# A chunked RWKV-7 scan: the state kept as 128x64 without its zero blocks, with the products on it made per head

## What is computed

```python
    def step(S, inp):
        r_t, k_t, v_t, kk_t, a_t, w_t = inp
        sa = jnp.einsum('bhij,bhj->bhi', S, kk_t)
        S = (S * w_t[:, :, None, :] - sa[..., None] * (kk_t * a_t)[:, :, None, :]
             + v_t[..., None] * k_t[:, :, None, :])
        return S, jnp.einsum('bhij,bhj->bhi', S, r_t)
```

## Time and profile before

| | |
|---|---|
| median of 3 runs | 2623.42 us (2622.43 to 2625.33) |
| profiled execution | 2622.69 us |
| its span | 2620.5 us |
| mean granted TensorE clock | 0.946 |
| TensorE busy | 2308.7 us (88%) |
| VectorE busy | 1187.0 us (45%) |
| ScalarE busy | 790.7 us (30%) |
| GpSimd busy | 441.7 us (17%) |

### The profile page before, as it was taken

The page is one execution under the profiler, slowest core; times in us unless marked ns, Lnnn a source line. Parts: engine busy times, 40 slices in busy tenths (PEclk is TensorE's granted clock), DMA queues, the critical chain, the costliest instruction groups (busy, mean ns, idle before and its releaser), DMA issues. The chain is left out here.

```text
span 2620.5 us, 51046 instructions
## 1 busy us (share of the span) xinstructions
PE 2308.7 (88%) x21174; PEld 2102.2 (80%) x21174; DVE 1187.0 (45%) x2330; ACT 790.7 (30%) x1494; POOL 441.7 (17%) x239
## 2 busy tenths in 40 slices
PE   5999999999999999999999789999246637999996
PEld 4998989898988888899999777888223327999996
DVE  4244545444454545348898144444223425443223
ACT  4343333333332332122222344544111113232111
POOL 0000000000000000001100499999200000000000
PEclk8999999999999999999999899999668877999998
DMA  3321222222221212268775513221575632342232
GB/s 116 98 83 60 83 64 75 64 79 60 80 79 60 80 62 85 75 198 287 226 254 186 153 57 93 69 85 44 164 236 170 189 115 103 124 146 106 102 101 93
DMA packets 124556, 301.65 MB, mean 115 GB/s; under 512 B 24218, under 2 KB 37156, under 8 KB 118596
## 3 DMA queue, kind: packets, MB, share of 16 engines
q1 hardware_dynamic: 97972, 242.44, 29.1%
q0 software_dynamic: 7696, 32.78, 3.6%
q10 hardware_dynamic: 18688, 23.59, 2.8%
HBM read 261.55 MB, written 45.54 MB: 117 GB/s over the span
## 5 line engine op out<-in xcount | busy, mean ns | idle before, releaser
L177 PE MATMUL acc<-xh,w_hi 128*128 128x272 f32 x3008 | 670.5, 304 | 24.0 <-DVE xl L433 12.0
L177 PE MATMUL acc<-xh,w_lo 128*128 128x272 f32 x3008 | 624.8, 289 | 0.0
L177 PE MATMUL acc<-xl,w_hi 128*128 128x272 f32 x3008 | 623.8, 289 | 0.0
L177 PEld LDWEIGHTS acc<-xh,w_hi 128*128 128x128 f32 x3008 | 472.1, 190 | 76.0 <-issue 45.4
L177 PEld LDWEIGHTS acc<-xl,w_hi 128*128 128x128 f32 x3008 | 475.7, 190 | 0.0
L177 PEld LDWEIGHTS acc<-xh,w_lo 128*128 128x128 f32 x3008 | 473.4, 190 | 0.0
L160 DVE TENSOR_TENSOR w_lo<-w_raw,w_hi 128x1024 fp32r<-128x1024 f32 x166 | 203.2, 1224 | 412.6 <-ACT w_hi L152 411.5
L152 ACT ACTIVATE w_hi<-w_raw 128x1024 fp32r<-128x1024 f32 x188 | 198.5, 1056 | 301.1 <-PE acc L177 245.7
L1171 DVE SCALAR_TENSOR_TENSOR b_C<-b_rows,b_pos_s,b_C 128x512 f32<-128x512 f32 x240 | 162.4, 743 | 0.0
L893 PE MATMUL rbank<-m 64*64 64x64 f32 x3840 | 130.9, 220 | 1.1 <-DVE m L584 1.1
L893 PEld LDWEIGHTS rbank<-m 64*64 64x64 f32 x3840 | 118.8, 135 | 15.2 <-issue 3.8
(11 more groups left out here) (386 smaller groups left out, 3350.6 us busy)
## 6 DMA issues: line engine op xcount, KB each, us to landing
w_raw<-in_w_all SPq DMA_DIRECT2D x188, 512.0 KB, 3.6
b_rows<-in_cmp_rows SPq DMA_DIRECT2D x128, 256.0 KB, 3.7
d_kv<-in_sel_kv SPq DMA_DIRECT2D x128, 256.0 KB, 2.9
m_w<-in_w_mo SPq DMA_DIRECT2D x32, 1024.0 KB, 5.7
m_gates<-tmp_uT SPq DMA_DIRECT2D x16, 544.0 KB, 3.7
out_s_win<-in_win_in POOLq DMA_DIRECT2D x8, 1016.0 KB, 5.8
tmp_uT<-ub POOLq DMA_DIRECT2D x24, 272.0 KB, 2.3
tmp_uT<-ub ACTq DMA_DIRECT2D x23, 272.0 KB, 2.6
```

The source lines that it names most:

```text
L177: ins = self.nc.tensor.matmul(acc[:, c, 0:HALF], w[:, k % KH, :], x[:, k, c * HALF:(c + 1) * HALF], start=(k == 0 and m == 0), stop=(k == ...
```

## The change

S and Sd become 128x64: head 0's state on partitions 0 to 63, head 1's on 64 to 127, in the same columns. U is made by two products of 64 rows, one per head, into two PSUM banks (0 and 1 instead of 1). The state part of O is made per head too, and each stands ahead of its head's UV part. The new S takes one VectorE instruction instead of two. The final transpose of S gives 64x128, and the stores of `p_rwkv` read it so. Banks and gaps of all other jobs stay, so the place of every background piece does.

```diff
@@ PAIR_JOBS
-    PAIR_JOBS += [(f"U{_n}", 1, 1, "dve", 2), (f"O{_n}", 3, 1, "act", 1), (f"S{_n}", 0, 1, "dve", 0)]
+    PAIR_JOBS += [(f"U{_n}", 0, 2, "dve", 2), (f"O{_n}", 3, 1, "act", 1), (f"S{_n}", 0, 1, "dve", 0)]
@@ rwkv
-        S, Sd, S_nat = sb("S", [P, P]), sb("Sd", [P, P]), sb("S_nat", [P, P])
+        S, Sd, S_nat = sb("S", [P, CH]), sb("Sd", [P, CH]), sb("S_nat", [CH, P])
@@ GpSimd
-                    pool.dma_start(A["p_rwkv"][2 * i + h], S_nat[h * HD:(h + 1) * HD, h * HD:(h + 1) * HD]).then_inc(s_sent, 16)
+                    pool.dma_start(A["p_rwkv"][2 * i + h], S_nat[:, h * HD:(h + 1) * HD]).then_inc(s_sent, 16)
@@ VectorE
-                        in0=bank[0:CH, bank_of[i, f"U{n}"], 0:P].rearrange("p (h i) -> p h i", h=2), scalar=-1.0,
+                        in0=bank[0:CH, bank_of[i, f"U{n}"]:bank_of[i, f"U{n}"] + 2, 0:CH], scalar=-1.0,
                         in1=W2[:, :, n, :], op0=ALU.mult, op1=ALU.subtract).then_inc(ev_dve, 1)
@@
-                    for h, hp in enumerate((slice(0, CH), slice(CH, P))):
-                        last = stt(out=S[hp, h * CH:(h + 1) * CH], in0=bank[hp, bank_of[i, f"S{n}"], 0:CH],
-                                   scalar=last_p[hp], in1=Sd[hp, h * CH:(h + 1) * CH], op0=ALU.mult, op1=ALU.add)
-                    last.then_inc(ev_dve, 1)
+                    stt(out=S[:, :], in0=bank[:, bank_of[i, f"S{n}"], 0:CH], scalar=last_p, in1=Sd[:, :],
+                        op0=ALU.mult, op1=ALU.add).then_inc(ev_dve, 1)
@@ ScalarE
-                out(i, "S_out", S_nat[:, :], bank[:, bank_of[i, "S_out"], 0:P])
+                out(i, "S_out", S_nat[:, :], bank[0:CH, bank_of[i, "S_out"], 0:P])
@@ TensorE
-                    done(mm(bank[0:CH, bank_of[i, f"U{n}"], 0:P], mats["W1T"][:, n, :], S[:, :], start=True, stop=True))
+                    for h, hp in enumerate(H):
+                        ins = mm(bank[0:CH, bank_of[i, f"U{n}"] + h, 0:CH], mats["W1T"][hp, n, :], S[hp, :],
+                                 start=True, stop=True)
+                    done(ins)
@@
-                    mm(bank[:, b, 0:CH], S[:, :], KR[:, n, 1, :], start=True, stop=False)
                     for h, hp in enumerate(H):
+                        mm(bank[hp, b, 0:CH], S[hp, :], KR[hp, n, 1, :], start=True, stop=False)
                         ins = mm(bank[hp, b, 0:CH], UV[:, n, h * CH:(h + 1) * CH],
                                  G[:, h, n, CH:P], start=False, stop=True)
@@
-                done(nc.tensor.transpose(bank[:, bank_of[i, "S_out"], 0:P], S[:, :], ident[:, :]))
+                done(nc.tensor.transpose(bank[0:CH, bank_of[i, "S_out"], 0:P], S[:, :], ident[:, :]))
```

## The result

| | before | changed |
|---|---|---|
| median | 2623.42 us | 2651.91 us (2648.48 to 2657.03, 5 runs) |
| profiled execution | 2622.69 us | 2654.75 us |
| span | 2620.5 us | 2652.6 us |
| mean granted TensorE clock | 0.946 | 0.944 |

The changed kernel is slower: ratio 1.0113, 95% interval 1.0099 to 1.0126 (the two medians of the table alone give 1.0109). The forecast was 2648 us, 2637 to 2660.

The account below looks back on a forecast made before the run. TensorE, busy 117.2 of 120.9 us per pair, was taken to bound the kernel. O +31.6, U -4.1 and VectorE -2.5 sum to +25.0 us, giving 2648 us, range 2637 to 2660.

Parts of the forecast that it names:

- The price of a change of tile shape: In O on TensorE: each visit to another tile shape costs 0.14 us on top of its passes.
- a case with 4 rows against 128: Sample attention's L2110 (4 rows) against L2109 (128 rows), both 64 columns: source of the 0.14 us per visit.
- The visits of 0.25 us: In O: each visit with one 64-column product takes 0.14 + 2 x 0.055 = 0.25 us.
- the +0.39: O to S in the 25 chunks where TensorE waits ahead of O: 0.39 us longer each.
- forecast 0.56: O to S in the 39 chunks without a wait ahead of O: 0.56 us longer each.
- The rival of cheap row changes: In O, changing rows alone costs nothing extra: 2621.5 us, no change; chance 0.08.
- case in between: In O, neighbouring heads overlap after all: 2632 us; lies between the forecast and the cheap-rows rival.
- The rival that the changes are dearer still: In O, each shape change costs 0.20 us with the first weights, 11.5 us more: 2660 us; chance 0.09.
- 0.50 was forecast, from five chunks: U per head saves 0.10 us in the 5 chunks a pair where the saving reaches the end.
- -0.36 a pair forecast: VectorE's single S update (-0.29 us) and smaller Sd (-0.07), on the path once a pair.
- a lower clock in the stage: A lower granted TensorE clock in the scan would make it slower than forecast; no size given.

Follow-up runs that it names:

- o_alone: Kernel before the change with only O's state part made per head (64x64), each ahead of its head's UV part: 2662.43 us, ratio 1.0156.
- states_first: Changed kernel with O's two 64x64 state products next to each other, then the two UV products: 2614.39 us, ratio 0.9972.
- split_s: Changed kernel with the state update as two VectorE instructions of 64 partitions again: 2659.26 us, ratio 1.0149.
- state_early: Changed kernel with O's two state products issued directly behind U's, in the same 64x64 tile: 2602.81 us, ratio 0.9924.
- early_gap3: Changed kernel with O's state products directly behind U's and background pieces moved to O1, O4, O5 from U2, U5, U6: 2582.71 us, ratio 0.9845.
- o_tall: Kernel before with U per head and O's state part per head over all 128 rows, zeros included: 2612.12 us, ratio 0.9963.
- gap_after: Changed kernel with one background piece per pair moved from ahead of U2 to ahead of O1: 2638.67 us, ratio 1.0052.

## Why the prediction was right

- **The price of a change of tile shape** was the step on which all rested, taken from a case with 4 rows against 128. The visits of 0.25 us came out as forecast, and o_alone gives 4.12 us a pair where 3.97 was worked out. After a wait, O to the next job took 616.06 - 614.95 = 1.11 us instead of 604.68 - 603.96 = 0.72 (the latter two starts in the kernel before): the +0.39. Without one it grew by 0.59, forecast 0.56. The rival of cheap row changes fell with it. The rule that the Trainium skill gives in "TensorEngine Tiling (Array Packing)", Tiling Modes, is that a change of tiling mode drains TensorE; this case agrees: two shape changes fewer, in states_first, gave 3.9 us a pair. The prediction's case in between, that neighbouring heads overlap after all, could not come in the order of the change; states_first shows that they do overlap once they are neighbours. The rival that the changes are dearer still (0.20 a visit) fell by the 0.25 us steps.
- **U** saved 0.54 us a pair; 0.50 was forecast, from five chunks.
- **VectorE** was mis-sized: -0.36 a pair forecast. The update in one instruction gave 0.62, by split_s, and Sd takes 0.03 less (254 ns median instead of 286; no run tries it alone). I had called the update hidden in the chunks where UV waits for w_lo, and that was wrong by 0.11 us in each of three.
- **The sum of a pair**: 4.12 - 0.54 - 0.65 = 2.93, and the changed kernel's pair measures 2.93. Forecast was 3.11 (3.97 - 0.50 - 0.36).
- **The last pair** should have been 3.2 us longer by the forecast's terms (4 x 0.56 + 4 x 0.39 - 0.6) and is 2.3 longer, from its first U to its last job. The prediction left out a fifth wait there, ahead of the final transpose of S. It was 1.3 us (first line below, the kernel before) and is 0.4 (second line, the changed kernel); in o_alone, with VectorE's work as before, it is 0.7. So TensorE's extra time was partly hidden in it, where the prediction said that none would be.

```profile
PE rbank L973 <- DVE S L605: 1.3, 1, 1.3
```

```profile
PE rbank L974 <- DVE S L604: 0.4, 1, 0.4
```

- **The clock**: the text named a lower clock in the stage as something that would make it slower than forecast, and gave it no price. It came: 3 x 1.55 = 4.7 us. With it the scan grew by 27.3 us in the profiled execution, from its first U to its last job (25.0 forecast without any low clock, 22.7 measured without it).
- **The rest**, 4.4 us behind the scan, lies in the prompt attention in this execution. What sets the clock there from run to run was not tried; the median grew by 28.5, less than this execution's 32.1.

That the forecast of 2648 lies 4 us from the median owes something to errors of opposite sign: the scan without its low clock was taken 2.3 us too dear (0.18 of it in each pair, 0.9 in the last), and the clock's 4.7 us were left out. The mechanism was right; the closeness of the number is partly luck.

## What to carry to other kernels

Smaller matmuls are not cheaper by themselves: count how often the sequence changes the array's tile shape, and read the price of one change from start to start of neighbouring rows. Put products of one shape next to each other, even if some multiply zeros. Where a wait stands in a table of gaps, try to move filler work there before cutting the work around it; here that was worth 20 us (state_early to early_gap3). state_early was itself 20 us ahead of the kernel before, of which the cheaper U and state update are about 9 and the order of the products the rest.

## What the runs showed of the hardware that was not expected

- A visit to another tile shape costs 0.14 to 0.15 us beyond its passes, whether the rows change (0.25 us from L961 to L962 for two passes that need 0.11), the columns (0.26 from L959 to L961) or both (L948, 0.15). Products of different heads in one shape overlap even across jobs (630.69 and 630.70 above).
- The granted clock fell to half for 3.4 us in three to five of eight pairs when a wait of 1.3 us was followed by lone products of changing shape, though TensorE was busy by the profile from the end of the wait on; each fall cost 1.55 us. None fell with only one of the two present (states_first, o_tall and state_early have a wait of 1.2 to 1.4 us there, gap_after has the products and, in its first seven pairs, no wait above 0.85 us ahead of O). What picks the pairs is open.
- VectorE's UV instruction started 0.11 us later behind w_lo, after w_lo's end and not before it, in every kernel whose state update, the last instruction ahead of it to read PSUM, ended with one that starts at partition 64 (1.26 against 1.14 us after w_lo's start, in chunks 1, 4 and 5). That the start partition decides is a reading of the traces, not an experiment.
